# Norm sums ahead of the last product, squares behind each residual, high parts first, and a second set of weight buffers in one MLP

## The reference

```python
# first block, layers 1 and 2 (the context tokens only in layer 1)
m = mixer(x * (1 + sc1) + sh1)                 # w_in, three branches, gates, w_out
x = layer_norm(ALPHA * x + (1 + g1) * m)
f = (silu(h @ w_gate) * (h @ w_up)) @ w_down   # h = x * (1 + sc2) + sh2, hidden width 2816
x = layer_norm(ALPHA * x + (1 + g2) * f)
# second block, layer 1 a recurrent mixer, layer 2 a pooling mixer
x = x + gt_m * mixer2(modulate(rms_norm(x)))
x = x + gt_f * (relu(modulate(rms_norm(x)) @ w1) ** 2 @ w2)   # hidden width 4096
return rms_norm(x)
```

## Time and profile before

| | us |
|---|---|
| median of 3 runs | 2013.02 |
| lowest and highest | 2006.27, 2021.65 |
| the profiled execution | 2012.65 |
| its span | 2010.8 |
| mean granted TensorE clock in it | 0.967 of full |
| TensorE, VectorE, ScalarE, GpSimd busy | 1871.4, 1362.0, 851.5, 97.0 |

### The profile page before, as it was taken

How to read it: one execution, slowest core, us unless ns; L and a number is a source line. 1 busy time by engine, 2 the same in 40 slices (tenths; PEclk the granted TensorE clock), 3 DMA queues, 4 the chain that set the end, 5 groups by cost and what they waited for, 6 DMA issues and landing times.

```text
span 2010.8 us, 29426 instructions
## 1 busy us (share of the span) xinstructions
PE 1871.4 (93%) x11708; PEld 1622.8 (81%) x11708; DVE 1362.0 (68%) x2442; ACT 851.5 (42%) x1379; POOL 97.0 (5%) x86
## 2 busy tenths in 40 slices
PE   6999999999999999997999988899988899978998
PEld 4787667567878888886887857899987799978998
DVE  5762453764577787776656676778868778867665
ACT  3432463463252221224446454533358544444444
POOL 0000000000400000012000000100041000010000
PEclk8999999999989999998999999999979899988999
DMA  9553202202435568863842514578734557734553
GB/s 347 185 182 104 84 22 84 90 11 74 142 104 178 185 221 296 288 209 105 260 169 84 191 47 142 186 240 283 262 126 134 181 195 246 255 123 151 187 187 126
DMA packets 253960, 336.10 MB, mean 167 GB/s; under 512 B 5504, under 2 KB 223360, under 8 KB 253440
## 3 DMA queue, kind: packets, MB, share of 16 engines
q1 hardware_dynamic: 242784, 305.42, 45.9%
q10 hardware_dynamic: 11040, 28.80, 4.3%
HBM read 333.14 MB, written 1.05 MB: 166 GB/s over the span
## 4 chain that ended last, share of the span: by engine, by line
PE 73%; DVE 12%; DMA 6%; issue 4%; ACT 4%; POOL 0%; ACTq 0%; DVEq 0%; SPq 0%; POOLq 0%
PE ps L597 19%; PE ps L599 18%; PE ps L598 18%; DVE SL L556 3%; PE ps L1489 3%; DMA RAW<-in_w_ffn_gate 2%; ACT SH L550 2%; PE ps L1515 2%; PE ps L1499 2%; PE ps L1008 2%; PE ps L1404 1%; DMA RAW<-in_w_ffn_down 1%; DVE SIDE L470 1%; PE ps L1406 1%; PE ps L1405 1%
## 5 line engine op out<-in xcount | busy, mean ns | idle before, releaser
L556 DVE TENSOR_TENSOR SL<-RAW,SH 128x1024 fp32r<-128x1024 f32 (+2 forms) x448 | 521.8, 1167 | 324.2 <-ACT SH L550 321.7
L550 ACT ACTIVATE SH<-RAW 128x1024 fp32r<-128x1024 f32 (+2 forms) x448 | 442.5, 998 | 524.3 <-PE ps L599 247.7
L597 PE MATMUL ps<-AB,SH 128*128 128x256 f32 (+1 forms) x1856 | 603.0, 325 | 41.0 <-DVE AB L1145 25.5
L598 PE MATMUL ps<-AB,SH 128*128 128x256 f32 (+1 forms) x1856 | 596.8, 322 | 0.0
L599 PE MATMUL ps<-AB,SL 128*128 128x256 f32 (+1 forms) x1856 | 596.6, 321 | 0.0
L597 PEld LDWEIGHTS ps<-AB,SH 128*128 128x128 f32 x1856 | 355.7, 192 | 80.3 <-issue 32.5
L599 PEld LDWEIGHTS ps<-AB,SL 128*128 128x128 f32 x1856 | 356.5, 192 | 26.7
L598 PEld LDWEIGHTS ps<-AB,SH 128*128 128x128 f32 x1856 | 356.4, 192 | 25.9
L597 PE MATMUL ps<-HH,SH 128*128 128x256 f32 (+1 forms) x992 | 303.5, 306 | 13.2 <-DVE HL L942 7.0
L598 PE MATMUL ps<-HL,SH 128*128 128x256 f32 (+1 forms) x992 | 302.5, 305 | 0.0
L599 PE MATMUL ps<-HH,SL 128*128 128x256 f32 (+1 forms) x992 | 302.5, 305 | 0.0
(11 more groups left out here) (290 smaller groups left out, 2312.6 us busy)
## 6 DMA issues: line engine op xcount, KB each, us to landing
SIDE<-in_w_mod_t SPq DMA_DIRECT2D x67, 1024.0 KB, 7.2
RAW<-in_ffn_w SPq DMA_DIRECT2D x64, 1024.0 KB, 5.3
RAW<-in_w_in SPq DMA_DIRECT2D x44, 1024.0 KB, 5.4
RAW<-in_w_ffn_gate SPq DMA_DIRECT2D x22, 1024.0 KB, 6.6
RAW<-in_w_ffn_up SPq DMA_DIRECT2D x22, 1024.0 KB, 5.5
SIDE<-in_w_mod_t ACTq DMA_DIRECT2D x17, 1024.0 KB, 5.2
RAW<-in_w_ffn_down SPq DMA_DIRECT2D x16, 1024.0 KB, 6.9
RAW<-in_w_branch SPq DMA_DIRECT2D x24, 512.0 KB, 3.4
```

The source lines that it names most:

```text
L550: e.activation(SH[:, m, 0:kt, :], RAW[p][:, 0:kt, o:o + P], ACT.Copy).then_inc(K.up("weight_high"), 1)
L556: e.tensor_tensor(SL[:, m, 0:kt, :], RAW[p][:, 0:kt, o:o + P], SH[:, m, 0:kt, :].bitcast(F32), ALU.subtract).then_inc(K.up("weight_low"), 1)
L597: e.matmul(ps, SH[:, m, k, :], xh, start=k == 0, stop=False)
L598: e.matmul(ps, SH[:, m, k, :], xl, start=False, stop=False)
```

## The change

Four edits.

1. **Norm sums ahead.** In the last unit in front of a norm, TensorE sums tiles 0 to 6 (S1, S2, and without a mean the squares of tile 6 apart) before the last three matmuls of m = 3 (sums_ahead). It waits there for GpSimd's adds and, without a mean, for the square of tile 6. After the last product only tile 7 is left for pe_sums. The final norm keeps its order, except that the square of tile 7 comes in LastDown and before the scaling of tile 6.
2. **Squares behind each residual.** read_act of a Residual squares the tile that VectorE has just written (t = tile0 + m), waits for that X read, and stands on ScalarE ahead of the split of the next weights for this m. GpSimd adds tile 3 in the first of the two units.
3. **First step by high parts.** In a unit by k the step k = 0 is done for all four m with the high part of the input (eight matmuls) as soon as it is there (input_high), and the four matmuls with its low part follow.
4. **Two sets of weights in layer two's MLP.** Its 17 units load in turn into MACC ("spare") and RAW ("pair"), and a load waits for the splits of the unit two before. The first of them also waits until the branches are done with MACC. A table that is loaded into MACC after the MLP waits for the last of its splits.

```diff
@@ build
+    RAWS = [RAW, [MACC[:, 4 * p:4 * p + 4, :].rearrange("p a b -> p (a b)").rearrange("p (k c) -> p k c", c=2 * P) for p in range(2)]]
@@ class Unit
+        raw, pair, behind, over_branch, alone = RAW, "pair", 6, False, False
...
-                    e.wait_ge(sem["weight_low"], K.at("weight_low", 2 * p - 6))
-                e.dma_start(RAW[p][:, 0:self.kt, :], self.src(K, p)).then_inc(K.up(f"pair{p}_loaded", 16), 16)
+                    e.wait_ge(sem["weight_low"], K.at("weight_low", 2 * p - self.behind))
+                if self.over_branch:
+                    e.wait_ge(sem["hidden_low"], K.at("hidden_low"))
+                e.dma_start(self.raw[p][:, 0:self.kt, :], self.src(K, p)).then_inc(K.up(f"{self.pair}{p}_loaded", 16), 16)
...
+                if (m, k) == (3, self.kt - 1):
+                    self.sums_ahead(e, K)
+                if self.by_k and k == 0:
+                    if m == 0:
+                        self.high_first(e, K)
+                        waited = 0
+                    continue
...
+        def high_first(self, e, K):
+
+            c0, c1 = self.tokens
+            e.wait_ge(sem["input_high"], K.at("input_high", 1 - KT))
+            xh, xl = self.moving(0, 0, c0, c1)
+            for m in range(4):
+                e.wait_ge(sem["weight_low"], K.at("weight_low", m - 3))
+                reader, count = K.bank[self.bank0 + m]
+                e.wait_ge(sem[reader], K.value(reader, count))
+                ps = PS[self.bank0 + m][:, 0:c1 - c0]
+                e.matmul(ps, SH[:, m, 0, :], xh, start=True, stop=False)
+                e.matmul(ps, SL[:, m, 0, :], xh, start=False, stop=False)
+            e.wait_ge(sem["input_low"], K.at("input_low", 1 - KT))
+            for m in range(4):
+                e.matmul(PS[self.bank0 + m][:, 0:c1 - c0], SH[:, m, 0, :], xl, start=False, stop=False)
@@ stats_pool
-        for t in range(1, 3) if first else range(3, KT - 1 if mean else KT - 2):
-            if mean and t != 3:
+        for t in range(1, 4) if first else range(4, KT - 1 if mean else KT - 2):
+            if mean:
                 total(t)
             add_square(t)
-        if mean and first:
-            total(3)
@@ class Residual
         def read_act(self, e, K, m):
 
-            t = self.tile0 + m - 1
-            if not self.stats or t < 0:
+            t = self.tile0 + m
+            if not self.stats:
                 return
             c0, c1 = self.tokens
-            e.wait_ge(sem["dve_read"], K.at("dve_read", m))
+            e.wait_ge(sem["dve_read"], K.at("dve_read", m + 1))
+            if t == KT - 1:
+                e.activation(NT[:, 1, c0:c1], X[:, t, c0:c1], ACT.Square).then_inc(K.up("last_squared"), 1)
+                return
...
+        def sums_ahead(self, e, K):
+
+            if not self.stats or self.first:
+                return
+            c0, c1 = self.tokens
+            norm = Norm(tokens=self.tokens)
+            reader, count = K.bank[6]
+            e.wait_ge(sem[reader], K.value(reader, count))
+            e.wait_ge(sem["square_added"], K.at("square_added", 3 if self.mean else 2))
+            if self.mean:
+                e.wait_ge(sem["pool_done"], K.at("pool_done", 3))
+                norm.add_columns(e, 6, 4, S1[:, c0:c1], True, False)
+            norm.add_columns(e, 6, 0, S2[:, c0:c1], not self.mean, False)
+            if not self.mean:
+                e.wait_ge(sem["tile_squared"], K.at("tile_squared", 3))
+                norm.add_columns(e, 6, 0, SQR[:, 0, c0:c1], False, False)
@@ class Norm
...
                 if self.mean:
+                    e.wait_ge(sem["dve_read"], K.at("dve_read"))
                     self.add_columns(e, 6, 4, X[:, KT - 1, c0:c1], False, False)
+                e.wait_ge(sem["last_squared"], K.at("last_squared"))
                 ins = self.add_columns(e, 6, 0, NT[:, 1, c0:c1], False, True)
...
-                    e.tensor_copy(high[:, k, c0:c1], a).then_inc(K.up("dve_done"), 1)
-                    e.wait_ge(sem["dve_done"], K.own("dve_done"))
+                    e.tensor_copy(high[:, k, c0:c1], a).then_inc(K.up("input_high"), 1)
+                    e.wait_ge(sem["input_high"], K.own("input_high"))
...
-            if not self.split and not self.summed and not self.paired:
-
-                e.wait_ge(sem["dve_read"], K.at("dve_read"))
-                e.activation(NT[:, 1, c0:c1], X[:, KT - 1, c0:c1], ACT.Square).then_inc(K.up("last_squared"), 1)
@@ sequence, layer two
+        if l == 1:
+            for j, unit in enumerate(seq[-17:]):
+                unit.raw, unit.pair = RAWS[(j + 1) % 2], ("pair", "spare")[(j + 1) % 2]
+                unit.behind, unit.over_branch, unit.alone = 10, j == 0, True
```

More of the change, by code:

```diff
@@ L542, in load @@
                 if K.s("products"):
-                    e.wait_ge(sem["weight_low"], K.at("weight_low", 2 * p - 6))
-                e.dma_start(RAW[p][:, 0:self.kt, :], self.src(K, p)).then_inc(K.up(f"pair{p}_loaded", 16), 16)
+                    e.wait_ge(sem["weight_low"], K.at("weight_low", 2 * p - self.behind))
+                if self.over_branch:
+                    e.wait_ge(sem["hidden_low"], K.at("hidden_low"))
+                e.dma_start(self.raw[p][:, 0:self.kt, :], self.src(K, p)).then_inc(K.up(f"{self.pair}{p}_loaded", 16), 16)
         def split_act(self, e, K, m, loads):
             p = m // 2
-            e.wait_ge(sem[f"pair{p}_loaded"], K.at(f"pair{p}_loaded", 16 * loads))
+            e.wait_ge(sem[f"{self.pair}{p}_loaded"], K.at(f"{self.pair}{p}_loaded", 16 if self.alone else 16 * loads))
             kt, o = self.kt, self.offs[m]
-            e.activation(SH[:, m, 0:kt, :], RAW[p][:, 0:kt, o:o + P], ACT.Copy).then_inc(K.up("weight_high"), 1)
+            e.activation(SH[:, m, 0:kt, :], self.raw[p][:, 0:kt, o:o + P], ACT.Copy).then_inc(K.up("weight_high"), 1)
         def split_dve(self, e, K, m, before=0):
@@ L555, in split_dve @@
             kt, o = self.kt, self.offs[m]
-            e.tensor_tensor(SL[:, m, 0:kt, :], RAW[p][:, 0:kt, o:o + P], SH[:, m, 0:kt, :].bitcast(F32),
+            e.tensor_tensor(SL[:, m, 0:kt, :], self.raw[p][:, 0:kt, o:o + P], SH[:, m, 0:kt, :].bitcast(F32),
                             ALU.subtract).then_inc(K.up("weight_low"), 1)
@@ L860, in add_square @@
         def add_square(t):
-            e.wait_ge(sem["tile_squared"], K.at("tile_squared", t + 1 if first else t - 2))
+            e.wait_ge(sem["tile_squared"], K.at("tile_squared", t + 1 if first else t - 3))
             if t > 1:
@@ L1028, in pe_sums @@
             c0, c1 = self.tokens
-            if K.s("square_added"):
+            n = c1 - c0
+            if self.paired:
                 e.wait_ge(sem["square_added"], K.at("square_added"))
[L1031 to L1041, removed]
+                reader, count = K.bank[6]
+                e.wait_ge(sem[reader], K.value(reader, count))
+                self.add_columns(e, 6, 0, S2[:, c0:c1], True, False)
                 self.add_columns(e, 6, 0, S2[:, n:2 * n], False, False)
@@ L2259, in build, with sums_ahead @@
     class LastDown(Down):
+        def sums_ahead(self, e, K):
+            pass
         def read_act(self, e, K, m):
@@ L2586, in build @@
     gelu[1].bank0 = 4
+    conv[0].alone = True
     seq += [LruBias(), conv[0], conv[1], Gates(), gelu[0], gelu[1], LruOut()]
```

16 lines of the change are left out of this document (7 added, 9 removed).

## The result

| us | before | after |
|---|---|---|
| median of ten runs each | 2011.93 | 2019.06 |
| lowest and highest | 2006.27, 2021.65 | 2012.99, 2025.71 |
| the profiled execution, its span | 2012.65, 2010.8 | 2017.79, 2015.9 |
| mean granted clock in it | 0.967 | 0.959 |

The ratio of the times is 1.0043, with a 95% interval of 1.0026 to 1.0061: slower by about 9 us (the two medians differ by 7.1), inside one per cent, and 2.6 us over the forecast of 2016.5.

A forecast was written before the change was run, and what follows sets the result against it. TensorE, busy 1871.4 of 2010.8 us, bounds the kernel; a weight-transfer circle bounds layer two's MLP. 2010.8 - 12 (second set) - 2.8 (high parts) + 18.3 (norms) = 2014.3 span, 2016.5 on the median; 8-in-10 range 2001 to 2029.

The forecast's parts named there:

- The round lags: In 256-column pairs before norms, X read, square, copy and low part take 3.05 us a round against TensorE's 2.72 a tile.
- rival 1: In the 256-column pairs before norms the round does not lag: 1994.3 us span, 1996.5 on the median; chance 0.12.
- the recurrent output and the next MLP: The norm's first vector operation comes 5.85 us later at the recurrent output, 3.85 later at the second block's first MLP.
- Layer two's two norms: From first X read to the norm's first vector operation: 5.1 us longer at its output, 4.9 at its last down units.
- then does the sums (eight passes, 1.05) and three matmuls (0.35): At layer two's output, TensorE waits for GpSimd's adds, then spends 1.05 us on sums and 0.35 on matmuls.
- Rival 3 (the clock): Longer TensorE pauses prolong half clock in the four 256-column norms, 1.5 to 2 us each: +7, 2023.5 us; chance 0.14.
- Layer one: Its two 512-column norms build no lag: first vector operation 1.85 us sooner at the first, 0.65 later at the second.
- The whole loss at norms: Changes at all norms, the last one included, sum to +18.3 us; bounds -1.75 and +20.8.
- High parts first: Units by k behind norms start 0.43 us (256 columns) or 0.75 (512) sooner; gain 2.8, bounds nothing and 5.
- The second set: In layer two's MLP, alternating RAW and MACC hides the 7.87 us weight transfer; gain 12, bounds 9.25 and 13.3.
- rival 2: In layer two's MLP the one queue is the limit, so the second set gives nothing: 2028.5 us; chance 0.1.
- the shared port pair: Two-input VectorE operations and GpSimd shut each other out; if they met in every pair, the norm loss reaches 20.8 us.

The follow-up runs named there:

- copy_first: The changed kernel with ScalarE copying the next weights' high part before squaring the tile, in units adding to X; 0.9952 of the kernel before, 2000.46 us.
- squares_behind: The changed kernel with norm sums ahead undone, all sums behind the last product again; 1.0005 of the kernel before, 2009.75 us.
- high_only: The kernel before with only the first step by high parts added; 0.9972 of the kernel before, 2003.5 us.
- changed: The changed kernel with all four edits, run again beside others on one chip; 1.0053 of the kernel before, 2020.39 us.
- pauses: Edits 3 and 4 alone, plus a TensorE wait before the 7th and 13th units of layer two's MLP; 0.9953 of the kernel before, 1999.41 us.
- sets_high: The changed kernel with edits 1 and 2 undone; 0.9943 of the kernel before, 1995.57 us; run again as high_sets_2, 0.9942.
- layer1_ahead: sets_high plus sums ahead and squares behind read and copy in the two 512-column norms; 0.9928 of the kernel before, 1991.69 us; again as ahead_512_2, 0.9924.

## Why the prediction was right, and where its steps were off

The time lay 2.6 us over the forecast, in its case and its range. As a change it was less close: +3.5 forecast, +7.1 by the medians and about +9 by the ratio. By its steps:

- *The round lags* (rival 1 was that it does not): right. Rounds are 3.11 us in place of 3.05, and the recurrent output and the next MLP came within 0.5 us of the working. `copy_first` gives the cause: with the copy ahead of the square 18.5 of the 23.7 us of the four pairs are gone.
- *Layer two's two norms*: under-sized, +5.1 and +4.9 against +6.7 and +6.3. The step that failed is "then does the sums (eight passes, 1.05) and three matmuls (0.35)". They ran behind a wait of 3.94 us, at half clock. Rival 3 (the clock), which I kept apart as a case with its own chance, belonged into the sum, as a part of a long wait inserted in TensorE's stream. Its place was wrong as well: it bites in front of V first, not only behind the norm.
- *Layer one*: the sum was near (-1.85 and +0.65 against -2.4 and +0.1), its parts were not. I took the gain from the sums ahead. `squares_behind` has V 39.81 and 38.67 behind the first read, against 41.62 and 40.47 with sums ahead and 44.03 and 40.38 before. So the early squares win 4.2 and 1.7, and the sums ahead give 1.8 back each time. The trace of before shows why:

```profile
547.76 3.48 PE L1008 MATMUL ps<-ONES,S 128*128 128x1 f32 x16 [2.07 <-POOL S L864]
```

TensorE waited 2.07 us for GpSimd's add of a late square, and the sums behind that wait ran 3.48 us where they take 1.84 (`squares_behind`). With the square one slot earlier neither is left. At the second norm the wait was 2.07 too, but the sums ran in 1.95, and so the early squares win less there.
- *The whole loss at norms*: from read to V the working adds up to 18.5 for the six norms of the table, the trace to 21.4.
- *High parts first*: 2.8 forecast. `high_only` has 0.10 to 0.46%, 2 to 9 us: right in sign, and 2.8 lies at the lower end of it. The stretches behind layer one's norms became 2.1 and 0.7 shorter, where I had given 0.75 and nothing; but in `changed`, the same kernel profiled again, they are 335.96 and 321.93 us, 0.7 shorter and 0.3 longer than before. So these two lengths do not show what the high parts are worth.
- *The second set*: mechanism right, rival 2 wrong: no DMA wait, no idle time of TensorE. The profiled gain of 7.4 in place of 12.6 is one of pace. In the profile of `changed`, with the same program at the fast pace, the stretch from V (1277.13) to the first read of the last pair (1448.50) is 171.4 us: 13.6 under before, so the 12.6 of the working was near.
- *What made the total fit*: I was 3 us short at the norms and 5 us too high on the second set, 8 together. On the other side stand 2 us more from the stretches behind layer one's norms, 1 from that behind the recurrent output, and the last stretch of the table, 4.5 shorter, in which before ran at the slow pace for 160 us and after did not. The closeness of the sum is partly that luck.

The Trainium skill (SBUF — State Buffer, on the shared port pair) was weighed on the loss: in the new order of the 256-column pairs GpSimd's last add ends at 1268.80 and VectorE's low part starts at 1268.79 and takes its usual 1.23 us. They hardly meet (for 0.04 us at most in layer two's two pairs), and that rule cost nothing there. In the kernel before they had met: four low parts of the same pair took 1.37 to 1.77 us under GpSimd's adds. In layer one of `squares_behind`, where an add of 128 x 512 (541.41, 1.30 long) lies over the low part of 541.78, that low part takes 2.02 us, 0.8 more for 0.93 of overlap: there the trace agrees.

## What to carry to other kernels

Where two engines hand a tile to each other, write down one whole round, from read to read, and hold it against the tile time of the engine that feeds them: a square of 0.4 us put between the two halves, with the X read that it waits for, cost 18.5 us over four norms more than the same square behind the hand-over. Work moved from behind the last product to in front of it only pays if it wasn't hidden there already. A long wait that it brings into TensorE's stream is to be priced with the clock that follows: behind 3.94 us it was 0.50 for 17 us, while behind the 1.32 us of `pauses` it stayed at 1.00. Profile a changed kernel twice before a difference of 4% in a stretch without a stall is explained by the change.

## What had not been expected: two paces at full clock

Matmuls of 256 columns, each with its weight load, came at one of two paces in stretches in which TensorE was never idle, both at granted clock 1.00: 0.1133 us each (355 in 40 us) or 0.1178 (342). These windows are from before, in the last MLP, from `changed`, in layer two's MLP and in the last one, and from after, in the last one:

```profile
1860.00:1900.00 40.00, 40.00 (x342) 40.00 (x341) 29.42 (x45) 17.03 (x22) 0.00 (x0) 1.00 0.59 188
```
```profile
1340.00:1380.00 40.00, 40.00 (x355) 40.00 (x354) 35.16 (x58) 17.85 (x22) 0.00 (x0) 1.00 0.90 298
...
1900.00:1940.00 40.00, 40.00 (x342) 40.00 (x341) 28.47 (x44) 17.68 (x22) 0.00 (x0) 1.00 0.61 189
```
```profile
1900.00:1940.00 40.00, 40.00 (x356) 40.00 (x354) 28.69 (x43) 17.05 (x22) 0.00 (x0) 1.00 0.58 185
```

The changed kernel was profiled twice: in one execution its layer two's MLP is slow and its last MLP fast, in the other it is the reverse. The two other kernels that were profiled twice differ in the same way: in the window from 1340 to 1380 us `sets_high` has 342 and then 355 matmuls (`high_sets_2`), `layer1_ahead` 355 and then 342 (`ahead_512_2`). So it is neither the second set of buffers nor the edit, nor the chip, since each of these two had its first execution on one chip and its second on another. It isn't the load of the DMA engines either: 355 stand beside a share of 0.90, and 342 beside 0.59 and 0.90. The pace keeps to a value for up to 1490 matmuls. It changed at pauses of TensorE (`pauses`; in after one of 1.0 us at 1294.99), and also at the border of two units where no idle time shows. There the timeline has a hitch: two matmuls start 0.21 us apart (before, 1301.11), and the pace is another from there on. A long MLP costs 6 to 6.7 us more at the slow pace (1315 to 1490 times 0.0045). That is more than the 2.8 us forecast for edit 3, and two or three long MLPs at one pace or the other would make most of the spread between executions of one kernel (2006 to 2022 before); only the profiled executions show their pace, so this is not shown. The Trainium skill (TensorE: Matmul & The Clock Gate, in the section on the measured gap of matmuls back to back) gives one fixed cost for each matmul beside its columns; these traces show two. Which of them a stretch takes, and why, stays open.
